# Eight experts' rows: one-hot products against indirect transfers on DRAM tables

## The reference, cut to what matters

```python
def moe_swiglu(x, w_router, w1, w3, w2):      # x: 256 x 1024
    logits = x @ w_router                      # 256 x 8
    top_logits, top_idx = lax.top_k(logits, 2)
    gates = softmax(top_logits)
    ...                                        # rows sorted by expert, in blocks of 128
    x_blocks = x_ext[tok_pad]                  # gather of rows
    def expert_block(xb, e):
        h = silu(xb @ w1[e]) * (xb @ w3[e])    # 128 x 3584
        return h @ w2[e]                       # 128 x 1024
    y = y * gate_pad[:, None]
    out = zeros.at[tok_pad].add(y)             # scatter-add of rows
```

## Time and profile before

| what | value |
|---|---|
| time, median of 3 runs | 2197.36 us |
| the three runs | 2199.22, 2197.36, 2196.7 us |
| span of the profiled execution | 2199.7 us |
| busy share: PE, DVE, ACT, POOL | 98%, 72%, 55%, 7% |
| chain that ended last | PE 87%, DVE 7%, issue 2%, ACT 2%, DMA 1% |
| DMA in the span | 537.25 MB, mean 244 GB/s |

### The profile page before, as it was taken

One profiled execution on the slowest core, in us unless ns is written; L12 is line 12 of the kernel. 1 busy time (PEld: TensorE's weight loads), 2 busy tenths in 40 slices (PEclk: granted clock), 3 DMA queues, 4 the chain that ended last, 5 costly groups with the idle time before them and its releaser, 6 DMA issues.

```text
span 2199.7 us, 31791 instructions
## 1 busy us (share of the span) xinstructions
PE 2150.1 (98%) x12075; PEld 1799.4 (82%) x12075; DVE 1594.4 (72%) x1644; ACT 1217.3 (55%) x1204; POOL 159.8 (7%) x232
## 2 busy tenths in 40 slices
PE   8999999999999999999999999999999999999998
PEld 7987888898778888888888888888788887877886
DVE  3676554576788988989898988989866429866453
ACT  4254443415467777777776777777664323655442
POOL 1200000310300000000000000000066010000000
PEclk9999999999899999999999999999999999999999
DMA  9134555422599999999999999999846554535552
GB/s 346 56 111 154 183 190 186 140 74 83 187 332 351 352 371 352 361 349 359 348 358 351 362 370 349 364 350 361 298 154 195 191 147 148 170 101 160 189 191 77
DMA packets 240787, 537.25 MB, mean 244 GB/s; under 512 B 18006, under 2 KB 120448, under 8 KB 240320
## 3 DMA queue, kind: packets, MB, share of 16 engines
q1 hardware_dynamic: 236560, 521.11, 67.0%
q0 software_dynamic: 3168, 9.07, 1.6%
q10 hardware_dynamic: 976, 5.91, 0.6%
HBM read 534.71 MB, written 1.31 MB: 244 GB/s over the span
## 4 chain that ended last, share of the span: by engine, by line
PE 87%; DVE 7%; issue 2%; ACT 2%; DMA 1%; DVEq 0%; SPq 0%; ACTq 0%
PE bank L1311 9%; PE bank L1313 9%; PE bank L1312 9%; PE bank L1452 8%; PE bank L1448 8%; PE bank L1449 8%; PE bank L1037 6%; PE bank L1475 4%; PE bank L1476 4%; PE bank L1480 4%; PE bank L1612 2%; PE bank L1035 2%; DVE weights_lo L2408 2%; PE bank L1420 1%; PE bank L1594 1%
## 5 line engine op out<-in xcount | busy, mean ns | idle before, releaser
L2408 DVE TENSOR_TENSOR weights_lo<-ring_data,weights_hi 128x2048 fp32r<-128x2048 f32 x336 | 760.3, 2290 | 93.4 <-ACT weights_hi L2089 91.8
L2089 ACT ACTIVATE weights_hi<-ring_data 128x2048 fp32r<-128x2048 f32 x336 | 637.9, 1919 | 171.9 <-DMA ring_data<-in_moe_w 170.9
L1448 PE MATMUL bank<-weights_hi,xg_hi 128*128 128x512 f32 x896 | 352.3, 393 | 2.6 <-DVE arena L2866 2.6
L1449 PE MATMUL bank<-weights_hi,xg_lo 128*128 128x512 f32 x896 | 349.5, 390 | 0.0
L2403 DVE TENSOR_TENSOR weights_lo<-ring_data,weights_hi 128x2048 fp32r<-128x2048 f32 x98 | 227.5, 2352 | 49.5 <-ACT weights_hi L1864 49.5
L1452 PE MATMUL bank<-weights_lo,xg_hi 128*128 128x512 f32 x896 | 240.5, 390 | 0.1
L1312 PE MATMUL bank<-weights_lo,xT_hi 128*128 128x512 f32 x584 | 229.2, 393 | 0.0
L1311 PE MATMUL bank<-weights_hi,xT_hi 128*128 128x512 f32 x520 | 206.4, 397 | 1.7 <-issue 0.7
L1313 PE MATMUL bank<-weights_hi,xT_lo 128*128 128x512 f32 x520 | 203.3, 391 | 0.0
L1448 PEld LDWEIGHTS bank<-weights_hi,xg_hi 128*128 128x128 f32 x896 | 168.5, 188 | 37.1 <-issue 3.0
L1452 PEld LDWEIGHTS bank<-weights_lo,xg_hi 128*128 128x128 f32 x896 | 168.7, 188 | 35.8 <-DVE weights_lo L2408 0.5
(11 more groups left out here) (514 smaller groups left out, 3227.8 us busy)
## 6 DMA issues: line engine op xcount, KB each, us to landing
ring_data<-in_moe_w SPq DMA_DIRECT2D x672, 512.0 KB, 4.4
ring_data<-in_ffn_w_in SPq DMA_DIRECT2D x88, 512.0 KB, 4.7
ring_data<-in_w_in SPq DMA_DIRECT2D x70, 512.0 KB, 4.6
ring_data<-in_ffn_w SPq DMA_DIRECT2D x66, 512.0 KB, 4.1
ring_data<-in_ffn_w_out SPq DMA_DIRECT2D x44, 512.0 KB, 4.0
ring_data<-in_w_out SPq DMA_DIRECT2D x24, 512.0 KB, 4.7
ring_data<-in_w_in SPq DMA_DIRECT2D x8, 396.0 KB, 4.1
ring_data<-in_w_in SPq DMA_DIRECT2D x8, 390.0 KB, 5.5
```

Source lines behind the costliest of these rows:

```text
L1448: mm(o, xg_hi[:, k, :], e_hi(at)[:, r], start=k == 0, stop=False)
L1449: mm(o, xg_lo[:, k, :], e_hi(at)[:, r], start=False, stop=False)
L2089: nc.scalar.activation(e_hi(at), ring_data[:, e_slot(at), :], ACT.Copy).then_inc(ring.hi_done, 1)
L2408: v.tensor_tensor(e_lo(at), ring_data[:, e_slot(at), :], e_hi(at), ALU.subtract).then_inc(ring.lo_done, 1)
```

## The change: what it does

Two tables in DRAM, `x_rows` and `y_rows`, of 384 rows of 1024 floats are added: 256 rows for the tokens, and 128 blank rows for slots that hold no token. Before the first turn POOL stores x in the one, ALPHA * x in the other, and zeros in the blank rows of both.

At down (1, 1) PE multiplies `Pm` with three columns (`find_slots`): token number less 256, one, and gate. DVE turns the result into a row number and a gate for each slot (`place_slots`; a slot without a token gets a blank row of its own). POOL then fetches the next expert's 128 rows from `x_rows` with an indirect DMA into what was the first tile of x, and at down (2, 0) PE transposes them (`turn_rows`), 8 transposes in place of the 16 products of `gather`. At the end of a turn ACT and DVE each write one half of the result, times the gate, to what was the second tile of x (`y_scaled`), and POOL adds its 128 rows to `y_rows` with an indirect DMA that accumulates. The transposes of `PG`, `weigh`, `scatter`, `add` and the zeros of the first turn go. The first gather and the last expert's scatter stay products; for the latter `yacc` is read back from `y_rows` in the last turn.

```diff
+    p = np.arange(P)[:, None]
+    t["slotcol"] = np.concatenate([p - T, p * 0 + 1, p + P - T, p * 0 + 1, -p, p + T], 1)
...
+        gather_at, scatter_at = sb("gather_at", [P, 1], I32), sb("scatter_at", [P, 1], I32)
+        x_rows, y_rows = (nc.dram_tensor(k, (T + CAP, D), F32, kind="Internal").ap() for k in ("x_rows", "y_rows"))
+        slotin, slotout = gtm[:, 0, 0:TT * 3].rearrange("p (j c) -> p j c", j=TT), eqm[:, 0, 0:3]
+        xg_rows, y_scaled = x[:, 0, :], x[:, 1, :]
...
+            def experts():
+
+                pool.wait_ge(sem("y_stored"), STORED)
+                pool.wait_ge(sem("npass_ready"), 1)
+                last = pool.value_load(npass_i[0:1, 1:2], min_val=E - 1, max_val=2 * E - 1)
+                with pool.Fori(0, last) as it:
+                    pool.wait_ge(sem("slots_ready"), it * 4 + 7)
+                    pool.sem_inc(sem("rows_asked"), 1)
+                    nc.gpsimd.indirect_dma_start(xg_rows, None, x_rows[:, :], bass.IndirectOffsetOnAxis(gather_at[:, 0:1], 0)).then_inc(sem("rows_loaded"), 16)
+                    pool.wait_ge(sem("y_out"), it * 2 + 4)
+                    pool.sem_inc(sem("rows_asked"), 1)
+                    nc.gpsimd.indirect_dma_start(y_rows[:, :], bass.IndirectOffsetOnAxis(scatter_at[:, 0:1], 0), y_scaled, None, compute_op=ALU.add).then_inc(sem("y_stored"), 16)
+                pool.wait_ge(sem("y_stored"), last * 16 + STORED)
+                pool.sem_inc(sem("rows_asked"), 1)
+                for j in range(TT):
+                    pool.dma_start(yacc[:, j, :], y_rows[P * j:P * j + P, :]).then_inc(sem("rows_loaded"), 16)
+
+            pool.wait_ge(sem("dve_stage"), stage("norm_rows2"))
+            for j in range(TT):
+                pool.dma_start(x_rows[P * j:P * j + P, :], x[:, j, :]).then_inc(sem("y_stored"), 16)
...
+            pool.wait_ge(sem("dve_stage"), stage("y_init"))
+            for j in range(TT):
+                pool.dma_start(y_rows[P * j:P * j + P, :], yacc[:, j, :]).then_inc(sem("y_stored"), 16)
+            pool.wait_ge(sem("y_stored"), 32 * TT)
+            pool.wait_ge(sem("gather_psum"), 2)
+            nc.gpsimd.memset(y_scaled, 0.0).then_inc(sem("pool_stage"), 1)
+            pool.wait_ge(sem("pool_stage"), stage("slots_blank"))
+            for rows in (x_rows, y_rows):
+                pool.dma_start(rows[T:T + CAP, :], y_scaled).then_inc(sem("y_stored"), 16)
+            experts()
...
+                def find_slots(b, n):
+
+                    pe.wait_ge(sem("perm_ready"), n)
+                    for j in range(TT):
+                        i = mm(bank[b][:, 0:3], Pm[:, j, :], slotin[:, j, :], start=j == 0, stop=j == TT - 1)
+                    i.then_inc(sem("slots_psum"), 1)
+
+                def turn_rows(it):
+
+                    pe.wait_ge(sem("rows_loaded"), it * 16)
+                    for b in range(2):
+                        for d in range(4):
+                            i = nc.tensor.transpose(bk(6 + b, 4, CAP)[:, d], xg_rows[:, P * (4 * b + d):P * (4 * b + d + 1)], ident)
+                        i.then_inc(sem("gather_psum"), 1)
...
-                        if part == ("up", 1, 4):
-                            pe.wait_ge(sem("ysb_ready"), it * 2 + 2)
-                            pe.wait_ge(sem("pgT_ready"), it + 1)
+                        if part == ("down", 0, 0):
+                            pe.wait_ge(sem("y_out"), it * 2 + 2)
                             pe.wait_ge(sem("moe_hT"), it * 4 + 1)
-                            scatter(0)
-                        if part == ("up", 1, 6):
-                            pe.wait_ge(sem("y_added"), it * 4 + 2)
-                            scatter(1)
                         if part == ("up", 2, 1):
-                            pe.wait_ge(sem("y_added"), it * 4 + 4)
                             turn_h(1)
                         if part == ("down", 1, 0):
                             pe.wait_ge(sem("moe_hT"), it * 4 + 2)
                         if part == ("down", 1, 1):
-                            pe.wait_ge(sem("pg_ready"), it + 1)
-                            for j in range(TT):
-                                i = nc.tensor.transpose(bk(6, TT, P)[:, j], PG[:, j, :], ident)
-                            i.then_inc(sem("pgT_psum"), 1)
+                            if is_last:
+                                for j in range(TT):
+                                    i = nc.tensor.transpose(bk(6, TT, P)[:, j], Pm[:, j, :], ident)
+                                i.then_inc(sem("slots_psum"), 1)
+                            else:
+                                find_slots(6, it + 2)
                         if part == ("up", 3, 1):
-                            pe.wait_ge(sem("pgT_ready"), it + 2)
-                            pe.wait_ge(sem("gslot_ready"), it + 1)
+                            pe.wait_ge(sem("slots_ready"), it * 4 + (5 if is_last else 7))
                             turn_h(2)
                         if part == ("down", 2, 0):
                             pe.wait_ge(sem("moe_hT"), it * 4 + 3)
                             if not is_last:
-                                gather(it + 1)
+                                turn_rows(it + 1)
...
+                pe.wait_ge(sem("dve_stage"), stage("slot_gates"))
+                find_slots(4, 1)
...
+                        if part == ("down", 3, 1) and not is_last:
+                            act.wait_ge(sem("slots_ready"), it * 4 + 4)
+                            act.wait_ge(ring.used, used)
+                            a_(y_scaled[:, 0:512], bank[4][:, :], ACT.Copy, "y_out", scale=gslot[:, 0:1])
...
+                    v.tensor_copy(slotin[:, :, 2], gate.rearrange("p j a e -> p j (a e)")[:, :, bass.ds(it, 1)].rearrange("p j o -> p (j o)"))
...
+                def place_slots(b, n):
+
+                    dve.wait_ge(sem("slots_psum"), n)
+                    o = bank[b][:, 0:3]
+                    v.tensor_copy(slotout[:, 0:2], o[:, 0:2]).then_inc(sem("slots_ready"), 1)
+                    v.tensor_copy(slotout[:, 2:3], o[:, 2:3])
+                    dve.wait_ge(sem("slots_ready"), n * 4 - 3)
+                    v.scalar_tensor_tensor(slotout[:, 0:1], slotout[:, 1:2], const("slotcol")[:, 4:5], slotout[:, 0:1], ALU.mult, ALU.add).then_inc(sem("slots_ready"), 1)
+                    dve.wait_ge(sem("slots_ready"), n * 4 - 2)
+                    v.tensor_scalar(gather_at[:, :], slotout[:, 0:1], const("slotcol")[:, 5:6], None, ALU.add).then_inc(sem("slots_ready"), 1)
+
+                def keep_slots(it):
+
+                    dve.wait_ge(sem("slots_ready"), it * 4 + 3)
+                    dve.wait_ge(sem("y_stored"), it * 16 + STORED)
+                    v.tensor_copy(scatter_at[:, :], gather_at[:, :])
+                    v.tensor_copy(gslot[:, :], slotout[:, 2:3]).then_inc(sem("slots_ready"), 1)
...
                             if not is_last:
                                 choose(it + 1)
-                        if part == ("up", 1, 4):
-                            add(it, 0)
-                        if part == ("up", 1, 6):
-                            add(it, 1)
...
-                            dve.wait_ge(sem("gslot_ready"), it + 1)
-                            v.tensor_scalar(chosen[:, :, :], gate_row[:, :, :], 0.0, None, ALU.is_gt).then_inc(sem("pgT_ready"), 1)
+                            keep_slots(it)
+                            if is_last:
+                                dve.wait_ge(sem("slots_psum"), it + 2)
+                                v.tensor_copy(chosen[:, :, :], bk(6, TT, P)).then_inc(sem("slots_ready"), 1)
+                            else:
+                                dve.wait_ge(sem("slots_ready"), it * 4 + 4)
+                                place_slots(6, it + 2)
...
+                        if part == ("down", 3, 1) and not is_last:
+                            dve.wait_ge(sem("slots_ready"), it * 4 + 4)
+                            dve.wait_ge(ring.used, n_moe + e_first + s + 1 + it * MOE_LOADS)
+                            v.tensor_scalar(y_scaled[:, 512:D], bank[5][:, :], gslot[:, 0:1], None, ALU.mult).then_inc(sem("y_out"), 1)
...
+                dve.wait_ge(sem("rows_loaded"), last * 16 + 16 * TT)
```

More of the change, by code:

```diff
@@ L145 @@
 LN_DONE = (0, 4, 6, 8, 12)
+STORED = 16 * 6
 def stage(name):
@@ L466, in two_block_kernel @@
         ar.at += D
-        Pm, PG, gate_row = ar(TT, CAP), ar(TT, CAP), ar(TT, P)
+        Pm = ar(TT, CAP)
         at_chosen = ar.at
@@ L1542, in moe @@
                 for q in range(2):
-                    pe.wait_ge(sem("ysb_ready"), last * 2 + 3 + q)
+                    pe.wait_ge(sem("ysb_ready"), 1 + q)
                     for j in range(TT):
@@ L2126, in turn @@
                             turned(1, it * 4 + 2)
-                        if part == ("down", 1, 1):
-                            act.wait_ge(sem("pgT_psum"), it + 1)
-                            a_(gate_row[:, :, :], bk(6, TT, P), ACT.Copy, "gslot_ready", accum_out=gslot[:, 0:1])
```

(23 more changed lines are left out.)

30 lines of the change are left out of this document (9 added, 21 removed).

## The result

The changed kernel takes 2161.7 us (median of four runs, 2160.1 to 2162.4), the kernel before 2197.0 us beside it: a ratio of 0.984 (95% interval 0.983 to 0.985), 35.3 us less. Forecast were 2165 us, with a range of 2157 to 2196. A second series gave 2161.7 us again.

The account below looks back on a forecast made before the run. PE was taken to bound a turn. Savings of 17.8 (scatter) and 18.8 (gather), less 2.0 and 0.9 (`find_slots`) and 1.5 (tables), gave 32.2 us: span 2167.5, median forecast 2165 us, main case 2161 to 2174, range 2157 to 2196.

Parts of the forecast that it names:

- The bound: In a turn of the experts PE is the bound, busy 123.60 of 123.70 us; a turn becomes 119.1 us.
- Gather: At down (2, 0), eight transposes of 0.80 us replace products of 3.48 us: 2.68 us in seven turns, 18.8 us saved.
- Scatter for `find_slots`: Ahead of up (1, 4) and (1, 6), scatter's removal saves 2.22 us a turn, 17.8 us; `find_slots` adds 0.29, 2.0 us.
- The tables: Before the first turn, 3 MB to the tables delay the first loads by 0 to 3 us, taken as 1.5.
- The fetch: New PE wait at down (2, 0): 14 us remain, landing takes 9.1 us, so hidden with 5 us to spare.
- The rival of a late fetch: Landing after more than 14 us makes PE wait at down (2, 0) in seven turns: 2200 to 2260 us; chance 0.11.
- The additions: Asked for at a turn's end, waited for at down (1, 1) some 57 us later: no plausible landing reaches that.
- three passes: Rival: additions load the DMA engines for table read, SBUF read and write: 126.9 us a turn, 2220 us; loss case, chance 0.09.
- The stalls of weights: Row bursts hold up weights 0 to 0.6 us a turn, against 5.5 us of room: 0 to 4 us, taken as nothing.
- The rival that took 0.96 of a turn as what the engines need: DMA engines need 118.8 us a turn, 122.8 with rows, over PE's 119.1: 2191 us, range 2174 to 2196; chance 0.16.
- The prediction's rival: HBM limit of about 358 GB/s for a core: 128.5 us a turn, some 2231 us; DMA bound with loss, chance 0.09.
- The stages outside: Sign of being wrong: the stages outside the experts change by more than 3 us.

Follow-up runs that it names:

- the spread copies: Changed kernel plus 6.3 MB of plain DRAM copies in each of seven turns, issued as six pairs at six slots of a turn: 2206.4 us.
- the run with no margin: Changed kernel with the fetch held back until PE finished up (3, 3), the slot just ahead of the transposes: 2229.1 us, ratio to before 1.015.

## Why the prediction was right, point by point

- **The bound.** PE sets the turn before and after. Predicted were 119.1 us a turn, measured 118.92. The kernel that gave PE the gather back got longer by 2.48 us a turn.
- **Gather.** Predicted 2.68 us a turn, measured 2.48 by the kernel that puts it back. Scatter for `find_slots` was 2.22 - 0.29 = 1.93 and measured 2.32. Here the sum took the scatter from two places of two turns, and PE's wait of 1.4 us for DVE's `add` in another (0.23 a turn) was not in it; the rest of the difference was not followed. That the two misses nearly cancel is luck: 4.61 against 4.80 us, which over seven turns is 1.3 us.
- **`find_slots`.** 0.36 us instead of 0.43. The one ahead of the first turn was to take 0.9 us at half clock and took 0.36 at the full clock.
- **The tables.** Taken at 1.5 us. From the start of the gather to PE's first product in the loop it is 30.98 us instead of 30.45, 0.5 us more with that `find_slots` in it, so the tables cost next to nothing. With the line above this is 1.9 us. Together with the 1.3 us it makes the 3 us by which 35.3 exceeds 32.2.
- **The fetch.** The margin of 14 us was 13.95. The landing of 9.1 us, taken from plain transfers, was 6.5 to 8.7. The rival of a late fetch was priced too low: I counted the wait, but in the run with no margin it costs 9.0 us a turn for 7.0 us of wait.
- **The additions.** Landed after 7.5 to 11.8 us, where 57 were to be had. That they would load the engines with three passes has no support. A turn in which PE has no gap can't tell, but POOL's queue can: it took 3.6% of 16 engines' span for 20.61 MB, and 2.2% for 13.27 MB without the row transfers. That is about 66 engine-us per MB for fetches and additions together, near the 62 of plain transfers. With three passes for the additions it would be about twice that.
- **The stalls of weights.** Taken at nothing, with each burst holding weights up by at most about its own length. For the row transfers that was right: ACT's longest wait grew by 3.2 us, and PE had none. With 3.1 MB more behind the addition ACT waited 12.2 us, which is near the lengths of both together, and PE waited too.
- **The engines.** The rival that took 0.96 of a turn as what the engines need fails at that step: with the transfers left out the share is still 0.99, and 412 GB/s are possible in another run. My 385 GB/s, "level with PE", from 2 us at the start, was too low as a limit as well. By the Trainium skill, "DMA: Bandwidth & Descriptors", Specifications, the 358 GB/s for a core are a stack's 716 GB/s divided by two cores. The prediction's rival took this share for a ceiling of a core that runs alone, which it isn't here: the turn of the changed kernel has 378 GB/s, and the spread copies 412.
- **The stages outside.** They were to change by less than 3 us, and differ by 4.9 in the two profiles, so this sign of being wrong was met by the number. It was a bad sign: two profiles of the changed kernel differ by 4.7 us ahead of the gather alone, and the clock rows give an estimated 4 us behind the experts and 1.6 ahead of them. From the gather to the last scatter product the profiles differ by 35.1 us, as the medians do.

A version that beats the changed kernel did not come out of this. PE has no gap in a turn, and the transfers cost it 0.2 us.

## What to carry to other kernels

Where one engine has no gap, work taken off it comes back almost in full, if what replaces it lands ahead of its use: count that margin from the issue, and compare it with a landing in the same traffic. A DMA share near 1.00 doesn't show a bound while weights are fetched ahead; only a wait on the engine that needs them does. Spread over a turn, 3.1 MB more hid at 405 GB/s; the same bytes in one burst cost 7.7 us, while 1.05 MB hid in one burst. Waits on TensorE of 4.7 and 7.0 us cost the wait and a stretch at half the clock behind it. And before a difference in an unchanged stage is explained, compare two profiles of the same kernel there.

## What I had not expected of the hardware

- One core alone moved 412 GB/s over a whole turn of 125 us, with a busy share of 1.03 (and 405 over a turn without a gap on TensorE, at 1.02).
- An indirect fetch of 128 rows of 4 KB takes 2.24 us on POOL and lands after 6.5 to 8.7 us; an accumulating one takes 2.84 us and lands after 7.5 to 11.8 us. The fetch is in the range of the plain 512 KB transfers before, 3.8 to 9.1 us; the median addition, 10.5 us, is above it.
- After waits of 7 us TensorE's granted clock fell to 0.50 for a stretch, in a loop in which it had been 1.00.
